# Decay products of an HGRN2 head as 32-column blocks, and two FFN weight groups prepared ahead of the norm

## What is computed

```python
h = rmsnorm(x, norm_pre_mix) * (1 + sc_m) + sh_m
proj = h @ w_in                          # columns: HGRN2 q, f, i, g | attention q, k, v | indexer
...
gc = cumsum(log f) within a chunk        # per head: 4 heads, 128 key features, 128 value features
A[t, s] = sum_k q[t, k] * k[s, k] * exp(gc[t, k] - gc[s, k])   # for s <= t
o = A @ v + (state of earlier chunks)
...
x = x + gt_m * rmsnorm(y, norm_post_mix)
h = rmsnorm(x, norm_pre_ffn) * (1 + sc_f) + sh_f
gate, up = split(h @ w_ffn_in)           # 2816 columns each
y = (silu(gate) * up) @ w_ffn_out
x = x + gt_f * rmsnorm(y, norm_post_ffn)
```

## Time and profile before

| | |
|---|---|
| median of the runs (lowest to highest) | 803.05 us (802.88 to 803.44) |
| the profiled execution's own time | 805.04 us |
| its span, first to last instruction | 803.3 us |
| mean granted TensorE clock, share of full speed | 0.976 |
| busy: PE (TensorE matmul), PEld (its weight loads) | 758.8 us, 584.6 us |
| busy: DVE (VectorE), ACT (ScalarE), POOL (GpSimd) | 408.1 us, 283.4 us, 11.4 us |
| DMA moved | 88.02 MB, 110 GB/s on average |

### The profile page before, as it was taken

One profiled execution on the slowest core, in us unless ns is written; L12 is line 12 of the kernel. 1 busy time (PEld: TensorE's weight loads), 2 busy tenths in 40 slices (PEclk: granted clock), 3 DMA queues, 4 the chain that ended last, 5 costly groups with the idle time before them and its releaser, 6 DMA issues.

```text
span 803.3 us, 10163 instructions
## 1 busy us (share of the span) xinstructions
PE 758.8 (94%) x3554; PEld 584.6 (73%) x3554; DVE 408.1 (51%) x782; ACT 283.4 (35%) x463; POOL 11.4 (1%) x39
## 2 busy tenths in 40 slices
PE   4889999999999889998997999999999999999995
PEld 3555477777866576665885888888888888888884
DVE  3857669797988525427347332222333225344344
ACT  6345452534233233244257233322233333112123
POOL 5000000000000000000000000000000000000000
PEclk9899999999999989997998999999999999999998
DMA  9935015243343150552410432233333233423202
GB/s 310 347 88 150 1 45 167 73 136 102 106 134 107 28 179 19 165 204 84 160 50 27 131 100 84 80 102 104 104 104 91 77 94 123 139 80 103 78 1 105
DMA packets 103845, 88.02 MB, mean 110 GB/s; under 512 B 2980, under 2 KB 93192, under 8 KB 103816
## 3 DMA queue, kind: packets, MB, share of 16 engines
q1 hardware_dynamic: 103816, 87.65, 35.6%
HBM read 85.55 MB, written 2.10 MB: 109 GB/s over the span
## 4 chain that ended last, share of the span: by engine, by line
PE 84%; DVE 9%; issue 2%; DMA 2%; ACT 1%; SPq 1%; DVEq 0%; ACTq 0%
PE ps L1240 45%; PE ps L1261 21%; PE ps L1346 3%; PE ps L1453 2%; PE ps L1291 2%; PE ps L1521 1%; PE ps L1431 1%; DMA w_raw<-in_w_in 1%; DVE w_lo L779 1%; PE ps L1496 1%; PE ps L1580 1%; PE ps L1516 1%; PE ps L1588 1%; DVE score L1002 1%; DVE top L997 1%
## 5 line engine op out<-in xcount | busy, mean ns | idle before, releaser
L1240 PE MATMUL ps<-h_hi,w_hi 128*128 128x512 f32 x576 | 235.2, 408 | 1.1 <-DVE h_lo L832 1.1
L1240 PE MATMUL ps<-h_hi,w_lo 128*128 128x512 f32 x576 | 225.1, 391 | 0.0
L1240 PE MATMUL ps<-h_lo,w_hi 128*128 128x512 f32 x576 | 225.0, 391 | 0.0
L779 DVE TENSOR_TENSOR w_lo<-w_raw,w_hi 128x1024 fp32r<-128x1024 f32 (+1 forms) x110 | 128.7, 1187 | 168.8 <-ACT w_hi L434 168.6
L434 ACT ACTIVATE w_hi<-w_raw 128x1024 fp32r<-128x1024 f32 (+1 forms) x110 | 110.5, 1026 | 97.4 <-PE ps L1261 91.7
L1240 PEld LDWEIGHTS ps<-h_hi,w_hi 128*128 128x128 f32 x576 | 108.5, 188 | 43.5 <-issue 21.7
L1240 PEld LDWEIGHTS ps<-h_hi,w_lo 128*128 128x128 f32 x576 | 108.4, 188 | 23.6
L1240 PEld LDWEIGHTS ps<-h_lo,w_hi 128*128 128x128 f32 x576 | 108.7, 189 | 20.5 <-issue 1.0
L1261 PE MATMUL ps<-w_hi,h_hi 128*128 128x512 f32 x240 | 94.8, 395 | 0.8 <-DVE mix L1138 0.8
L1261 PE MATMUL ps<-w_lo,h_hi 128*128 128x512 f32 x240 | 94.0, 392 | 0.0
L1261 PE MATMUL ps<-w_hi,h_lo 128*128 128x512 f32 x240 | 93.9, 391 | 0.0
(11 more groups left out here) (223 smaller groups left out, 696.6 us busy)
## 6 DMA issues: line engine op xcount, KB each, us to landing
w_raw<-in_w_ffn_in SPq DMA_DIRECT2D x44, 512.0 KB, 4.0
w_raw<-in_w_in SPq DMA_DIRECT2D x28, 512.0 KB, 6.4
w_raw<-in_w_ffn_out SPq DMA_DIRECT2D x22, 512.0 KB, 3.6
adaw<-in_w_ada SPq DMA_DIRECT2D x20, 512.0 KB, 5.0
act<-in_w_ada SPq DMA_DIRECT2D x12, 512.0 KB, 9.0
res<-in_x SPq DMA_DIRECT2D x8, 512.0 KB, 4.8
adaw<-in_w_ada SPq DMA_DIRECT2D x4, 1024.0 KB, 5.3
act<-in_w_ada SPq DMA_DIRECT2D x4, 1024.0 KB, 5.2
```

The lines of the kernel that those rows point to most:

```text
L779: V.tensor_tensor(w_lo[slot][:, 0:n], w_raw[slot][:, 0:n], w_hi[slot][:, 0:n].bitcast(f32), ALU.subtract).then_inc(lo_ok, 1)
L1240: last = mm(ps[bank][0:rows, :], a, b, start=(k == 0 and n == 0), stop=(k == KT - 1 and n == 2))
```

## The change

1. **Levels.** Levels 0 to 5 form only the 32x32 blocks on the diagonal: for each token tile four products of 32 weight columns with 32 moving columns, block j into output partitions 32j to 32j + 31, in 128 columns of the bank instead of 512. Level 6 forms two such blocks a tile (j = 0, 2, moving columns one block ahead), level 7 one of 64x64.
2. **Masks and copies.** VectorE's multiply and predicated copies work on 128 columns (`blk`, a new 128x128 tile) with compact masks of 32 columns. ScalarE copies the four strips of `blk` into the diagonal blocks of `at_diag` after level 5. The zeros are now written once: GpSimd fills `at_diag`, after a wait for the start's adaLN products and sines, and ScalarE waits for it ahead of the heads. GpSimd also cuts the compact masks, eight small copies. VectorE waits at level 0 of a head for the previous head's block copies, TensorE ahead of the output product for this head's.
3. **FFN entry.** ScalarE splits group G_FIN ahead of the last tile's `y_stats` and group G_FIN + 1 ahead of its `row_stats`; VectorE subtracts the first ahead of the last `post_norm`, the second ahead of the last `norm_rows`. TensorE takes both groups block by block, each block for both, and starts when block 1 is there. In the loop ScalarE's split stands before SiLU.

```diff
@@ -95,6 +95,7 @@
         silu_pad = sb("silu_pad", KT * 32)
         gate_ffn = sb("gate_ffn", D_MODEL)
         masks = sb("masks", 5 * P)
+        block_masks = sb("block_masks", 6 * 32)
         ident = sb("ident", P)
         ones = sb("ones", P)
         dup = sb("dup", P)
@@ -141,6 +142,7 @@
         ik, ikw, r_tmp = part(res, 2048), part(res, 2560), part(res, 3072)
         r_tmp2 = part(res, 4608)
         relu = [part(res, 3584), part(res, 4096), r_tmp, r_tmp2]
+        blk = part(res, 5120, P)
         pt = part(res, 0, 2048)
         aq, ak, av, av_tok = part(res, 2048), part(res, 2560), part(res, 3072), part(res, 3584)
         p_off = [4096, 4224, 4480, 4864]
...
@@ -422,7 +424,15 @@
 
             for m in range(5):
                 level_mask(m)
+            for j in range(4):
+                rows = slice(32 * j, 32 * j + 32)
+                step(pool.tensor_copy(block_masks[rows, 0:32], ident[rows, rows]))
+                step(pool.tensor_copy(block_masks[rows, 32:192].rearrange("p (m c) -> p m c", m=5),
+                                      masks[rows, :].rearrange("p (m c) -> p m c", m=5)[:, :, rows]))
             pool.sem_inc(masks_ok, 1)
+            pool.wait_ge(ada_used, START_ADA)
+            pool.wait_ge(sin_ok, 4)
+            pool.memset(at_diag, 0.0).then_inc(at_zero, 1)
 
 
         @block.scalar
@@ -569,15 +579,20 @@
             def level_32(h):
 
                 sc.wait_ge(lvl_mm, h * LEVELS + 7)
+                pv = ps[2][:, 0:P].rearrange("p (c t) -> p c t", c=TT)
+                sc.activation(at_diag[0:32, :, 32:64], pv[0:32, :, :], ACT.Copy)
+                sc.activation(at_diag[64:96, :, 96:128], pv[64:96, :, :], ACT.Copy).then_inc(outer_out, 1)
                 sc.wait_ge(lvl_out, h * 6 + 6)
-                pv = ps[2][:, :].rearrange("p (c t) -> p c t", c=TT)
-                sc.activation(at_diag[0:32, :, 32:64], pv[0:32, :, 32:64], ACT.Copy)
-                sc.activation(at_diag[64:96, :, 96:128], pv[64:96, :, 96:128], ACT.Copy).then_inc(outer_out, 1)
+                bv = blk.rearrange("p (c t) -> p c t", c=TT)
+                for j in range(4):
+                    rows = slice(32 * j, 32 * j + 32)
+                    last_copy = sc.activation(at_diag[rows, :, rows], bv[rows, :, :], ACT.Copy)
+                last_copy.then_inc(blk_out, 1)
 
             def level_64(h):
                 sc.wait_ge(lvl_mm, h * LEVELS + 8)
-                pv = ps[3][:, :].rearrange("p (c t) -> p c t", c=TT)
-                sc.activation(at_diag[0:64, :, 64:128], pv[0:64, :, 64:128], ACT.Copy).then_inc(outer_out, 1)
+                pv = ps[3][:, 0:2 * P].rearrange("p (c t) -> p c t", c=TT)
+                sc.activation(at_diag[0:64, :, 64:128], pv[0:64, :, :], ACT.Copy).then_inc(outer_out, 1)
 
             def outer_levels(h):
 
@@ -654,6 +669,7 @@
             hg_i(0)
             hg_g(0)
 
+            sc.wait_ge(at_zero, 1)
             with sc.Fori(0, HG_HEADS - 1) as h:
                 hg_body(h, False)
             hg_body(HG_HEADS - 1, True)
@@ -736,25 +752,26 @@
             for k in range(4, KT):
                 split_hi(k % 4, U_OUT[k % 4] + 1, G_OUT + k - 3)
             for t in range(TT):
+                if t == TT - 1:
+                    split_hi(0, U_FIN[0], G_FIN - 3)
                 y_stats(0, t)
                 if t == 0:
                     continue
                 row_stats(1, t - 1)
+            split_hi(1, U_FIN[1], G_FIN - 2)
             row_stats(1, TT - 1)
 
-            split_hi(0, U_FIN[0], G_FIN - 3)
-            split_hi(1, U_FIN[1], G_FIN - 2)
             norm_hi(24, scale_ffn)
             with sc.Fori(0, FT // 2) as i:
                 for u in range(4):
+                    if u < 2:
+
+                        split_hi(u + 2, i + U_FIN[u + 2], i * 4 + (G_FIN + u - 1))
+                    else:
+                        split_hi(u - 2, i + (U_FIN[u - 2] + 1), i * 4 + (G_FIN + u - 1))
                     if u % 2 == 0:
                         sc.wait_ge(group_done, i * 4 + (G_FIN + u + 1))
                         sc.activation(silu_g[u // 2], ps[u][:, :], ACT.Silu).then_inc(silu_done[u // 2], 1)
-                    if u < 2:
-
-                        split_hi(u + 2, i + U_FIN[u + 2], i * 4 + (G_FIN + u - 1))
-                    else:
-                        split_hi(u - 2, i + (U_FIN[u - 2] + 1), i * 4 + (G_FIN + u - 1))
             nc.scalar.preload_act_table_set("natural_log_exp_and_others")
             with sc.Fori(0, FT // 4) as i:
                 for n, slot in enumerate((2, 3, 0, 1)):
@@ -1037,14 +1054,16 @@
                     for n in rounds:
                         find_eight(n)
 
-                    pv = ps[2 + st % 2][:, :].rearrange("p (c t) -> p c t", c=TT)
+                    pv = ps[2 + st % 2][:, 0:P].rearrange("p (c t) -> p c t", c=TT)
+                    bv = blk.rearrange("p (c t) -> p c t", c=TT)
+                    m = block_masks[:, None, min(st, 5) * 32:(min(st, 5) + 1) * 32]
                     if st == 0:
-                        V.tensor_tensor(at_diag, pv, ident[:, None, :].to_broadcast([P, TT, P]),
-                                        ALU.mult).then_inc(lvl_out, 1)
+                        if not (isinstance(h, int) and h == 0):
+                            ve.wait_ge(blk_out, h)
+                        V.tensor_tensor(bv, pv, m.to_broadcast([P, TT, 32]), ALU.mult).then_inc(lvl_out, 1)
                     elif st < 6:
-                        m = masks[:, None, (st - 1) * P:st * P].bitcast(u32).to_broadcast([P, TT, P])
                         wait_apart(lvl_out, h * 6 + st)
-                        V.copy_predicated(at_diag, m, pv).then_inc(lvl_out, 1)
+                        V.copy_predicated(bv, m.bitcast(u32).to_broadcast([P, TT, 32]), pv).then_inc(lvl_out, 1)
                     if st == 1:
                         if not (isinstance(h, int) and h == 0):
                             head_tail(h - 1)
@@ -1169,14 +1188,15 @@
             ve.wait_ge(x_again, 16 * TT)
             ve.wait_ge(gate_ok, 4)
             for t in range(TT):
+                if t == TT - 1:
+                    split_lo(G_FIN, 0)
                 post_norm(0, t, gate_mix)
                 if t:
                     norm_rows(1, t - 1)
+            split_lo(G_FIN + 1, 1)
             norm_rows(1, TT - 1)
             ve.wait_ge(scale_ok, 1)
-            split_lo(G_FIN, 0)
             norm_features(24, scale_ffn)
-            split_lo(G_FIN + 1, 1)
             def swiglu(i, v):
                 ve.wait_ge(silu_done[v], i + 1)
                 ve.wait_ge(group_done, i * 4 + (G_FIN + 2 * v + 2))
@@ -1447,10 +1467,17 @@
                     elif st >= 8:
                         te.wait_ge(outer_out, h * 4 + (st - 7))
                     bank = ps[2 + st % 2]
-                    if st < 8:
+                    if st < 7:
+                        ahead = 32 if st == 6 else 0
                         for t in range(TT):
-                            tt = slice(t * P, (t + 1) * P)
-                            last = mm(bank[:, tt], k_b[:, tt], q_f[:, tt], start=True, stop=True)
+                            for j in (0, 2) if st == 6 else range(4):
+                                at = t * P + 32 * j
+                                last = mm(bank[32 * j:32 * j + 32, t * 32:(t + 1) * 32], k_b[:, at:at + 32],
+                                          q_f[:, at + ahead:at + ahead + 32], start=True, stop=True)
+                    elif st == 7:
+                        for t in range(TT):
+                            last = mm(bank[0:64, t * 64:(t + 1) * 64], k_b[:, t * P:t * P + 64],
+                                      q_f[:, t * P + 64:(t + 1) * P], start=True, stop=True)
                     elif st == 8:
                         for b in range(2):
                             last = mm(bank[:, b * P:(b + 1) * P], k_b[:, 2 * b * P:(2 * b + 1) * P],
@@ -1492,6 +1519,7 @@
                 te.wait_ge(iv_ok, h + 1)
                 te.wait_ge(lvl_out, h * 6 + 6)
                 te.wait_ge(outer_out, h * 4 + 4)
+                te.wait_ge(blk_out, h + 1)
                 for s in range(TT):
                     last = mm(ps[7][:, s * P:SEQ], i_tok[:, s * P:(s + 1) * P],
                               att_hg[:, s * SEQ + s * P:(s + 1) * SEQ], start=(s == 0), stop=(s == TT - 1))
@@ -1615,11 +1643,16 @@
                 last.then_inc(xt_mm, 1)
 
             def fin_pass(i, first, last=False):
-                for u in range(4):
+                if first:
+                    te.wait_ge(lo_ok, G_FIN + 2)
+                    for k in range(KT):
+                        te.wait_ge(hlo_ok, KT + max(k + 1, 2))
+                        feature_step(k, 0, 0)
+                        feature_step(k, 1, 1)
+                for u in range(2 if first else 0, 4):
                     if not first:
                         te.wait_ge(act_ok[u // 2], i)
```

(11 more changed lines are left out.)

## The result

The changed kernel takes 791.24 us (median of four, 789.79 to 791.76), the one before in the same comparison 803.25 (802.88 to 804.0): a ratio of 0.9843, 95% interval 0.9827 to 0.9859. On the median that the prediction started from, this is 0.9843 x 803.05 = 790.4 us. The forecast was 795.1, the range 791.0 to 801.5: the direction was right, the gain half as large again as forecast, and the time just past the faster end. A second measurement of the changed kernel, beside other runs of the kernel before, gave 0.9855 (0.9828 to 0.9881), on the same base 791.4 us and just inside the range. So the size of the gain is clear, and on which side of 791.0 it lies is not.

What follows compares the result with a forecast made beforehand. The prediction took TensorE to bound the kernel (84% of the span). Terms -3.5 (levels), -1.3 (VectorE's waits), -2.0 (last head), -1.1 (FFN entry) sum to -7.9 us: 805.04 to 797.1, as a median 795.1; range 791 to 801.5.

Steps and rivals of the forecast that it cites:

- The price of the strips: TensorE levels in the heads: 0.12 to 0.14 us to go into the strips, 0.22 to come out, 0.35 together.
- ScalarE's and GpSimd's additions: ScalarE's four block copies per head, 1.1 us, hidden behind its wait for PE; GpSimd's copies and fill cost nothing.
- The norm: Norm ahead of the FFN: earlier weight splits fit idle gaps, PE starts first groups without stopping; -1.1 us.
- the bound of -2.6: Last head: largest gain allowed from shorter VectorE work in the levels, where -2.0 us was taken.
- part 1: TensorE's level products in the heads: small 32-column products in strips, body 0.5 us against 0.89; -3.5 us in heads 0 to 2.
- the transfer: Head 0: the second half of adaLN weights lands late, so savings of levels 2 and 3 are lost; head gives -0.9 us.
- the first term: Shorter TensorE level products in heads 0 to 2, -3.5 us in the sum.
- VectorE's waits: Heads 0 to 2: PE's one wait for VectorE, at level 7, goes (0.4 + 0.5 + 0.5); -1.3 us.
- rival C: Heads: levels as forecast, but DMA of adaLN weights or last head's PE replaces the waits; 799.5 us, chance 0.08.
- PE idle at the second adaLN product: Sign of a wrong forecast: TensorE waiting in a head at the second adaLN product; no size given.
- A: Heads' levels: strips follow each other slower than they issue, some 0.75 us a body; 800 us, chance 0.12.
- B: Heads' levels slower than before: each small pair costs whole load and stream, or own issue time; 824 us, chance 0.10.

Runs made afterwards that it cites:

- the levels only: Changed kernel with every edit ahead of the FFN taken back, level products, masks and copies kept; 792.83 us, ratio 0.9881.
- the long VectorE kernel: Changed kernel with an unused 320-element VectorE multiply behind each of a head's six masked operations; 797.0 us, ratio 0.9923.
- strip order: Changed kernel with products of levels 0 to 6 ordered strip by strip instead of rotating the strips; single run 798.56 us.
- the splits only: Changed kernel with early FFN weight splits kept, but TensorE taking the first two groups one after the other; one run 788.01 us.

## Why the prediction came out too small

**Right.** The price of the strips: 0.12 to go in (0.39 less the 0.27 of starts) and 0.2 to come out. VectorE's copies at 0.29 us. ScalarE's and GpSimd's additions cost nothing: behind its four block copies ScalarE still waits 0.4 us for TensorE in head 1, and GpSimd's fill ends at 51.7 us, long before head 0 starts at 107.6. The norm, by its own steps: both splits fit into the gaps, TensorE starts 0.1 us later behind the start of the last row sums (422.12 - 415.77 = 6.35, before 434.43 - 428.18 = 6.25) and then runs without a gap: -1.24 for -1.1. The last head's -2.84 lies just past the bound of -2.6, which was VectorE's share alone: with VectorE nearly as long as before, the last head is still 0.6 us shorter (33.90 against 34.48).

**The step that failed** is one sentence of part 1: "With 64 instructions a level takes at least 0.45 us to issue." The 7 ns of the earlier trace rows was the distance between weight loads of neighbouring strips. The prediction took it as the step of one queue of 64 loads and matmuls, and set this bound above its own streaming term, eight pairs a strip at 0.028 us, 0.22 in all. The runs show loads and matmuls side by side, 32 matmul starts within 0.26 us, and the pace of a strip as what counts: eight pairs, 52 ns to the second and 31 to 32 ns between the others. The body is 0.27 us, not 0.5. Level 6, which the prediction did price at 0.25, has that body too. With 0.27 in levels 0 to 5 and all else as the prediction counted it (levels 2 and 3 of head 0 lost to the transfer), a middle head gives 2.7 us and head 0 1.8, so the first term falls from -3.5 to -7.2 us, and the sum from -7.9 to -11.6, where 12.0 was measured. This one term is 3.7 of the 4.1 us that were missing.

**Smaller ones that nearly cancel.** With -7.2 for the levels and -1.3 for VectorE's waits, heads 0 to 2 should have given 8.5 us. They gave 7.9 and 8.5 in the two profiles of the change, 8.9 with the levels only: right within the spread, but not head by head. Head 0 gave 3.0 and 2.8 where the corrected sum has 2.2, since the transfer held it up by only 0.2 to 0.3 us. Heads 1 and 2 gave 2.4 to 3.0 where it has 3.2. In them level 7's wait, forecast to vanish, is still 0.2 us, and the transfer, seen as a bound in head 0 only, takes up to 0.7 us in some profiles. That is a part of rival C, and one of the prediction's signs of being wrong, "PE idle at the second adaLN product". The bound on VectorE was also put down too low: it was counted as the 0.5 us of wait in the trace, but what a resource next in line is worth depends on how much faster the first one gets (the long VectorE kernel: 5.4 us, where 1.3 + 2.0 was forecast).

**The rivals.** A (0.75 us a body) and B (over 0.9) are out for the kernel as built; strip order comes near A, with 0.83 us a level and so a body of 0.71. The Trainium skill, page "TensorE: Matmul & The Clock Gate", section "Wait — 56ns, not 53.3ns?", states about 25 ns between starts at the least. With the strips read as above, the runs agree within one strip (31 to 32 ns). Across strips they don't (6 to 7 ns), and the 62 ns for a matmul decoded in microcode were not seen: 32 were over in 0.46 us.

## What to carry to other kernels

Small products pay when they rotate through the column strips: count the pairs of load and matmul in the fullest strip, here 32 ns each for 32 moving columns, plus 0.3 us to go in and come out, and let the strips change in the innermost loop. Fewer pairs in fewer strips gain nothing: 16 pairs in two strips took as long as 32 in four. When a bound falls by some us, don't price the next resource by the wait that the old trace shows, but by how far it would now lag: add up both engines' work between two of their meetings. A step that is moved later to close a wait has a due time of its own; look for its first reader before moving it.

## What was not expected of the hardware

Stages that no edit touches differ between profiles by up to 6 us: attention with the output projection took 159.95 to 166.21 us in twelve profiles. Busy times of two stretches of it (columns as above), in the kernel after and then in the one with the splits only:

```profile
276.00:282.00 6.00, 3.54 (x30) 3.28 (x28) 3.39 (x19) 1.54 (x2) 0.00 (x0) 0.91 0.96 283
282.00:288.00 6.00, 5.71 (x28) 5.74 (x29) 0.75 (x2) 1.41 (x3) 0.00 (x0) 0.53 0.00 0
```
```profile
276.00:282.00 6.00, 3.24 (x29) 3.08 (x28) 4.14 (x20) 0.63 (x1) 0.00 (x0) 1.00 0.72 189
282.00:288.00 6.00, 5.03 (x33) 3.74 (x31) 1.24 (x2) 2.39 (x4) 0.00 (x0) 1.00 0.00 0
```

Behind a stretch in which TensorE was busy 3.54 of 6 us, the granted clock is at 0.53, nearly all of it at the lower level (1.2 GHz); in the other kernel, behind 3.24 busy of 6, it stays at 1.00 (2.4 GHz). Why one fell and the other did not is open. It matters for reading: a stage's own length settles an edit of 1 us that the medians of a few runs cannot. The edits of the FFN entry (-1.3 us in their stage, ratio 0.9998) are the example. It does so only where the stage itself is steady: head 2 of the changed kernel took 35.89 us in one profile and 35.32 in another, so 0.5 us in one head of one profile settles nothing.
